# A bias strip on ScalarE's queue, and an output stage finished by column halves: a hybrid decoder layer on one core

## The reference

```python
def _output(h, a_out, b_out, c_out, w_out, g_post):
    y = jnp.concatenate([a_out, b_out, c_out], axis=-1) @ w_out
    return h + _rms_norm(y, g_post)

def _rms_norm(x, g):
    xf = x.astype(jnp.float32)
    y = xf * lax.rsqrt(jnp.mean(xf * xf, axis=-1, keepdims=True) + EPS)
    return (y * g.astype(jnp.float32)).astype(x.dtype)

# before it: u = rms_norm(h, g_pre) @ w_in, split into the inputs of three mixers:
#   A: attention (compressed, selected, window branches) with a relative position bias
#      rel_bias[_t5_bucket(distance)] on every logit
#   B: GLU -> causal depthwise conv of 31 taps -> group norm over channels -> swish -> pointwise
#   C: causal conv of 4 taps -> gates -> linear recurrence over time
```

## Time and profile before

| | us |
|---|---|
| median of 3 runs | 1036.57 (1035.59 to 1037.96) |
| the profiled execution, its own time | 1041.16 |
| its span, first to last instruction | 1039.3 |
| TensorE matmul busy | 949.7 (91%) |
| VectorE busy | 598.8 (58%) |
| ScalarE busy | 374.9 (36%) |

### The profile page before, as it was taken

The page is one execution under the profiler, slowest core; times in us unless marked ns, Lnnn a source line. Parts: engine busy times, 40 slices in busy tenths (PEclk is TensorE's granted clock), DMA queues, the critical chain, the costliest instruction groups (busy, mean ns, idle before and its releaser), DMA issues.

```text
span 1039.3 us, 14529 instructions
## 1 busy us (share of the span) xinstructions
PE 949.7 (91%) x5469; PEld 586.3 (56%) x5469; DVE 598.8 (58%) x1112; ACT 374.9 (36%) x842; POOL 90.7 (9%) x88
## 2 busy tenths in 40 slices
PE   3999999997999999988999999998788989899996
PEld 2665665664666657665666666666454655544442
DVE  4388789999979869754555555577333233212222
ACT  4111253010212010347758667566254454310111
POOL 1011110000001111000020201211311000000000
PEclk9999999998999999999999999999899999999999
DMA  8333641043332554518000000000445755512210
GB/s 301 122 122 114 218 155 40 20 76 87 121 143 93 202 213 142 196 65 271 2 2 2 1 2 1 2 2 1 198 188 226 295 205 213 211 40 81 81 50 31
DMA packets 26734, 117.83 MB, mean 113 GB/s; under 512 B 2809, under 2 KB 11147, under 8 KB 20043
## 3 DMA queue, kind: packets, MB, share of 16 engines
q0 software_dynamic: 7056, 68.16, 17.7%
q1 hardware_dynamic: 18069, 45.75, 13.1%
q10 hardware_dynamic: 1551, 3.14, 1.0%
HBM read 108.07 MB, written 13.29 MB: 117 GB/s over the span
## 4 chain that ended last, share of the span: by engine, by line
PE 71%; DVE 8%; issue 5%; DMA 4%; ACT 4%; DVEq 3%; PEld 3%; SPq 2%; ACTq 0%; POOL 0%; PEldq 0%; POOLq 0%
PE PS L838 23%; PE PS L1825 12%; PE PS L1512 6%; PE PS L1502 6%; PE PS L1525 5%; PE PS L1713 3%; PE PS L1705 3%; PE PS L811 3%; PE PS L1541 2%; DMA main<-in_w_tiles_dram 2%; PEld PS L1757 2%; DVE main L611 2%; DMA main<-in_cmp_v_dram,row 1%; SPq L1030 1%; DVEq L747 1%
## 5 line engine op out<-in xcount | busy, mean ns | idle before, releaser
L838 PE MATMUL PS<-main 128*128 128x352 f32 (+1 forms) x1056 | 332.6, 474 | 7.0 <-DMA main<-in_w_tiles_dram 7.0
L838 PEld LDWEIGHTS PS<-main 128*128 128x128 f32 x1056 | 202.6, 193 | 128.9 <-DMA main<-in_w_tiles_dram 7.6
L1825 PE MATMUL PS<-main 128*128 128x512 f32 (+1 forms) x288 | 125.7, 599 | 0.8 <-DVEq L1689 0.8
L1353 ACT ACTIVATE main<-PS,main 128x512 f32<-128x512 f32 (+3 forms) x192 | 104.4, 566 | 0.7 <-DVE main L1395 0.7
L1345 ACT ACTIVATE main<-PS 128x512 f32<-128x512 f32 (+1 forms) x138 | 73.8, 578 | 77.9 <-PE PS L1512 77.2
L1825 PEld LDWEIGHTS PS<-main 128*128 128x128 f32 (+1 forms) x288 | 53.4, 186 | 72.3 <-issue 72.3
L434 ACT ACTIVATE main<-PS 128x384 f32<-128x384 f32 x24 | 11.8, 490 | 227.6 <-PE PS L838 219.1
L649 DVE SCALAR_TENSOR_TENSOR main<-main,par 128x1022 f32<-128x1022 f32 (+16 forms) x66 | 83.8, 1270 | 5.3 <-issue 0.4
L608 DVE TENSOR_TENSOR main<-main 128x1024 f32<-128x1024 f32 x64 | 75.4, 1220 | 11.7 <-DMA main<-in_cmp_k_dram,row 7.3
L1512 PE MATMUL PS<-cst,main 128*128 128x128 f32 x528 | 76.5, 286 | 3.4 <-ACT main L1353 3.2
L611 DVE TENSOR_TENSOR main<-main 128x1024 f32<-128x1024 f32 (+2 forms) x96 | 75.0, 781 | 7.2
(11 more groups left out here) (305 smaller groups left out, 1058.4 us busy)
## 6 DMA issues: line engine op xcount, KB each, us to landing
main<-in_w_tiles_dram SPq DMA_DIRECT2D x24, 512.0 KB, 4.0
main<-in_x_prompt_dram SPq DMA_DIRECT2D x16, 512.0 KB, 4.8
out_dram<-main SPq DMA_DIRECT2D x12, 512.0 KB, 2.6
main<-in_w_out_dram SPq DMA_DIRECT2D x1, 4096.0 KB, 12.0
diag<-in_win_k_dram SPq DMA_DIRECT2D x8, 256.0 KB, 10.2
diag<-in_win_v_dram SPq DMA_DIRECT2D x8, 256.0 KB, 11.6
out_dram<-in_win_k_dram SPq DMA_DIRECT2D x1, 2016.0 KB
out_dram<-in_win_v_dram SPq DMA_DIRECT2D x1, 2016.0 KB
```

The lines of the kernel that those rows point to most:

```text
L838: last = pe.matmul(bank(3 * s + j)[:, 0:w], ring[:, s, k * P:(k + 1) * P], xT[:, k, t0:t0 + w], start=(k == 0), stop=(k == KD - 1))
L1353: last = act.activation(prob[:, k % 2, g, h * nk_ * P:(h + 1) * nk_ * P], score_set(k, g)[:, h * nk_ * P:(h + 1) * nk_ * P], ACT.Exp, scal ...
L1825: last = pe.matmul(bank(2 * (n % 2) + h)[0:w, :], proj[:, MIX[k], n * P:n * P + w], wo[:, k, h * 512:(h + 1) * 512], start=(k == 0), stop= ...
```

## The change

It has two parts. The strip's store and its skewed read are issued by ScalarE instead of SyncE: the store after the copies of step 3, the read after those of step 5.

The output stage is written anew. The order of tiles is prompt 0 to 6, samples, prompt 7. A prompt tile is signalled, squared, multiplied with `g_post` and finished by halves of 512 columns; the product with `g_post` no longer holds the root and stands ahead of it (into `yb`), and the last operation of a half does the root and the sum with x in one. The sample tile is put on halves of the array's columns: each k has two matmuls of 64 stationary columns, whose results go to partitions 0 to 63 and 64 to 127 of one bank, so that 64 rows x 1024 become 128 x 512. Its sums of squares are then halves of a row's sum on two partitions; four matmuls of one column with pieces of the identity ("fold") add them, between the two halves of the last tile.

```diff
-        def sp_strip(sp):
-            sp.wait_ge(startup_evac, 4)
-            sp.dma_start(scratch["strip"], strip[0:H, :].rearrange("h (o c) -> h o c", o=1).to_broadcast([H, P, SKEW])).then_inc(strip_out, 16)
-
-        def sp_skew(sp):
-            sp.wait_ge(strip_out, 16)
-            sp.dma_start(diag[:, 1:, :], scratch["skewed"]).then_inc(strip_in, 16)
+        def act_strip(act):
+            act.wait_ge(startup_evac, 4)
+            act.dma_start(scratch["strip"], strip[0:H, :].rearrange("h (o c) -> h o c", o=1).to_broadcast([H, P, SKEW])).then_inc(strip_out, 16)
+
+        def act_skew(act):
+            act.wait_ge(strip_out, 16)
+            act.dma_start(diag[:, 1:, :], scratch["skewed"]).then_inc(strip_in, 16)
...
+        OUT = [0, 1, 2, 3, 4, 5, 6, 8, 7]
+        HALVES = [1 if n == NT else 2 for n in OUT]
+        DONE = [sum(HALVES[:m]) for m in range(10)]
...
+            sp.wait_ge(SEM["wvused"], 5)
+            for h in range(2):
+                sp.dma_start(gpost_s[S * h:S * (h + 1), :], dram["g_post"][:, h * 512:(h + 1) * 512].to_broadcast([S, 512])).then_inc(SEM["ld_gp"], 16)
+            for m in range(9):
+                for h, (here, there) in enumerate(x_parts(m, True)):
+                    if h < HALVES[m]:
+                        sp.wait_ge(SEM["y_out"], DONE[m] + h + 1)
+                    sp.dma_start(there, here).then_inc(y_st[m % 3], 16)
...
         def pe_output(pe):
             pe.wait_ge(SEM["ld_wo"], 16)
             pe.wait_ge(SEM["dpair"], 5)
...
+            for m, n in enumerate(OUT):
+                if m >= 2:
+                    pe.wait_ge(SEM["y_gain"], DONE[m - 1])
+                if n < NT:
+                    for h in range(2):
+                        for k in range(KD):
+                            last = pe.matmul(bank(2 * (m % 2) + h), proj[:, MIX[k], n * P:(n + 1) * P], wo[:, k, h * 512:(h + 1) * 512],
+                                             start=(k == 0), stop=(k == KD - 1))
+                        last.then_inc(SEM["y_ps"], 1)
+                        if h == 0 and m > 0 and OUT[m - 1] == NT:
+
+                            pe.wait_ge(SEM["y_sq"], DONE[m])
+                            for o in range(2):
+                                for a in range(2):
+                                    last = pe.matmul(bank(4)[S * o:S * (o + 1), 0:1], ident[:, S * a:S * (a + 1)], ssq[:, 0:1], start=(a == 0), stop=(a == 1))
+                            last.then_inc(SEM["y_fold"], 1)
+                else:
                     for k in range(KD):
...
+                        for h in range(2):
+                            last = pe.matmul(bank(2 * (m % 2))[S * h:S * (h + 1), :], proj[:, MIX[k], T:TOK], wo[:, k, h * 512:(h + 1) * 512],
+                                             start=(k == 0), stop=(k == KD - 1))
+                    last.then_inc(SEM["y_ps"], 1)
...
+                dve.wait_ge(SEM["y_sq"], DONE[m] + 1)
+                if n == NT:
+                    gain(0)
+                    dve.wait_ge(SEM["y_fold"], 1)
+                    dve.tensor_scalar(root, bank(4)[:, 0:1], 1.0 / D, EPS, ALU.mult, ALU.add).then_inc(SEM["y_ms"], 1)
+                else:
+                    one, two = ssq[:, 1 + 2 * (m % 2):2 + 2 * (m % 2)], ssq[:, 2 + 2 * (m % 2):3 + 2 * (m % 2)]
+                    dve.tensor_scalar(root, one, 1.0 / D, EPS, ALU.mult, ALU.add)
+                    gain(0)
+                    dve.wait_ge(SEM["y_sq"], DONE[m] + 2)
+                    dve.drain()
+                    dve.scalar_tensor_tensor(root, two, 1.0 / D, root, ALU.mult, ALU.add).then_inc(SEM["y_ms"], 1)
+                    gain(1)
+                dve.wait_ge(SEM["y_rt"], m + 1)
+                dve.reciprocal(root, root)
+                dve.wait_ge(xo_ld[b], 32 * (m // 3 + 1))
                 dve.drain()
...
+                for h in range(HALVES[m]):
+                    x = xo[:, b, h * 512:(h + 1) * 512]
+                    dve.scalar_tensor_tensor(x, yb[:, m % 2, h * 512:(h + 1) * 512], root, x, ALU.mult, ALU.add).then_inc(SEM["y_out"], 1)
```

More of the change, by code:

```diff
@@ L1785, in program, with x_parts @@
         gpost = late[:, 0:D]
+        gpost_s = late[:, D:D + 512]
         xo = carve(X0, 3 * D).rearrange("p (b n) -> p b n", b=3)
[L1787 to L1796, removed]
+        yb = carve(X0 + 3 * D, 2 * D).rearrange("p (b n) -> p b n", b=2)
+        junk = carve(X0 + 5 * D, 512)
+        OUT = [0, 1, 2, 3, 4, 5, 6, 8, 7]
+        HALVES = [1 if n == NT else 2 for n in OUT]
+        DONE = [sum(HALVES[:m]) for m in range(10)]
+        def x_parts(m, out):
+            n, b = OUT[m], m % 3
+            if n < NT:
+                full = (outs[0][0] if out else dram["x_prompt"])[n * P:(n + 1) * P, :]
+                return [(xo[:, b, h * 512:(h + 1) * 512], full[:, h * 512:(h + 1) * 512]) for h in range(2)]
+            full = outs[1].rearrange("b t d -> (b t) d") if out else dram["x_sample"]
+            return [(xo[S * h:S * (h + 1), b, 0:512], full[:, h * 512:(h + 1) * 512]) for h in range(2)]
         def sp_output(sp):
@@ L1803, in sp_output @@
             sp.wait_ge(SEM["vused"], 4)
[L1804 to L1812, removed]
+            for m in range(3):
+                for here, there in x_parts(m, False):
+                    sp.dma_start(here, there).then_inc(xo_ld[m], 16)
+            sp.wait_ge(SEM["wvused"], 5)
[6 more added lines that the diff above has]
+                    sp.dma_start(there, here).then_inc(y_st[m % 3], 16)
+                if m + 3 < 9:
+                    sp.wait_ge(y_st[m % 3], 32 * (m // 3 + 1))
+                    for here, there in x_parts(m + 3, False):
+                        sp.dma_start(here, there).then_inc(xo_ld[m % 3], 16)
             for b in range(3):
-                sp.wait_ge(y_st[b], 48)
+                sp.wait_ge(y_st[b], 96)
         def pe_output(pe):
@@ L1829, in act_output @@
+                    last.then_inc(SEM["y_ps"], 1)
         def act_output(act):
             act.wait_ge(SEM["vused"], 4)
[L1831 to L1834, removed]
+            for m, n in enumerate(OUT):
+                for h in range(HALVES[m]):
+                    act.wait_ge(SEM["y_ps"], DONE[m] + h + 1)
                     act.drain()
[L1836 to L1839, removed]
+                    sq = ssq[:, 0:1] if n == NT else ssq[:, 1 + 2 * (m % 2) + h:2 + 2 * (m % 2) + h]
+                    act.activation(junk, bank(2 * (m % 2) + h), ACT.Square, accum_out=sq).then_inc(SEM["y_sq"], 1)
+                act.wait_ge(SEM["y_ms"], m + 1)
+                act.activation(rstd[:, m:m + 1], rstd[:, m:m + 1], ACT.Sqrt).then_inc(SEM["y_rt"], 1)
@@ L1856, in program, with gain @@
-        yb = carve(X0 + 4 * D, 2 * D).rearrange("p (b n) -> p b n", b=2)
+            dve.wait_ge(SEM["ld_gp"], 48)
+            for m, n in enumerate(OUT):
+                b = m % 3
+                root = rstd[:, m:m + 1]
+                def gain(h):
+                    g = gpost_s if n == NT else gpost[:, h * 512:(h + 1) * 512]
+                    dve.tensor_tensor(yb[:, m % 2, h * 512:(h + 1) * 512], bank(2 * (m % 2) + h), g, ALU.mult).then_inc(SEM["y_gain"], 1)
+                dve.wait_ge(SEM["y_sq"], DONE[m] + 1)
[14 more added lines that the diff above has]
+                dve.wait_ge(xo_ld[b], 32 * (m // 3 + 1))
+                dve.drain()
+                for h in range(HALVES[m]):
+                    x = xo[:, b, h * 512:(h + 1) * 512]
+                    dve.scalar_tensor_tensor(x, yb[:, m % 2, h * 512:(h + 1) * 512], root, x, ALU.mult, ALU.add).then_inc(SEM["y_out"], 1)
```

25 lines of the change are left out of this document (4 added, 21 removed).

## The result

The changed kernel took 1029.14 us (median of 12 runs, 1024.96 to 1033.34), the kernel before 1037.38 beside it (12 runs, 1033.80 to 1044.88): ratio 0.9907, 95% interval 0.9882 to 0.9932. It is faster, by 0.9%. A ratio compares runs of the kernel's faster state alone, and need not be the quotient of the medians beside it. The forecast of 1029.8 was hit. In the trace the output stage came out near its price; the strip's price of 0 held for the profile it was read from, and not for others of the same kernel.

What follows compares the result with a forecast made beforehand. The prediction took VectorE's convolution to bound the projections and TensorE the output stage. Strip 0, TensorE's output work -5.86, tail -0.96 and last store 0 sum to -6.8 us: from 1036.57 to 1029.8, range 1026.8 to 1033.0.

Steps and rivals of the forecast that it cites:

- Part one: 0: Projections: moving the strip's transfers removes TensorE's 7.04 us weight-tile wait but gains 0, because VectorE's convolution covers it.
- the price without the cover, 9.2: Projections: without VectorE's convolution as cover, removing the tile wait would gain 9.2 us, 7.0 of wait and 2.2 of clock.
- it can move by 0.1 us at most: Third var matmul, issued at 290.27 behind a chunk ending at 290.25; VectorE frees its bank at 290.17, limiting any gain.
- Its +1.6: Part one's upper bound: the new wait lowers TensorE's clock again in the last chunk before 296.6, costing up to 1.6 us.
- The new wait: Projections, at `pe_mean`: TensorE waits about 4 us for VectorE at 257 to 261, in place of the tile wait.
- the last two rivals: Projections' clock: low again in the last chunk, 1031.4 us (chance 0.04); or at 1.2 GHz through the new waits, 1055.5 (0.02).
- The sign by which the forecast was to be wrong: Projections: VectorE's long wait for L884 ending more than 0.5 us away from 297.2 would show the forecast wrong.
- The sample tile: -6.65: Output stage: matmuls on two column halves run together, so the sample tile takes 7.18 us instead of 13.83.
- the rule of the Trainium skill: Output stage rival: column halves overlap partly, 1.59 times, sample tile 8.7 us, kernel 1031.3 us; chance 0.06.
- The fold: +0.79: Output stage, TensorE: four added matmuls, 8 instructions, cost 0.49 plus 0.30 us for the array's shape; bounds 0.3 and 1.28.
- The tail: -0.96: From the last tile's square to the last store's issue: 3.37 us instead of 4.33, including 0.20 for hops.
- The last store: 0: From the last store's issue to the span's end: no change from 3.35 us, bounds -0.7 and +0.35.

Runs made afterwards that it cites:

- e3: The kernel before with 10 of the 31 taps of convolution B left out, strip still on SyncE's queue; 1048.42 us, 1.0018 of the kernel before.
- e4: The kernel before with 10 of 31 convolution B taps left out and the strip's two transfers on ScalarE's queue; 1037.00 us, 0.9883 of the kernel before.
- e2: The changed kernel with the strip's two transfers back on SyncE's queue, so the new output stage alone; 1037.94 us, 0.9920 of the kernel before.
- e11: The kernel before, unchanged, profiled again; 37.31 us from L721 to the end of VectorE's long wait, against 36.32 in the first profile.
- e12: The kernel before, unchanged, profiled once more; 37.01 us from L721 to the end of VectorE's long wait, span 1052.6 us.
- e1: The kernel before with only the strip's two transfers moved to ScalarE's queue, output stage as before; 1041.25 us, 0.9954 of the kernel before.
- e9: The changed kernel, unaltered, run and profiled again on another chip; 1039.18 us, 0.9936 of the kernel before there (1045.29).
- e5: The changed kernel with both halves of the sample tile on the same 64 columns of TensorE; 1046.24 us, 0.9966 of the kernel before.
- e7: The changed kernel with TensorE's wait for the last decode pair moved from the output stage's start to the sample tile; 1035.37 us, 0.9885 of the kernel before.

## Why the prediction was right, step by step

**Part one: 0.** Right in the profile it was made from (36.32 and 36.30), and the price without the cover, 9.2, was right (9.1 in e3 and e4), its clock part by two errors: two of the four chunks behind the wait have 384 columns (5.16 us from start to start, against 4.73 for 352), so at full clock the 64 instructions take some 19.9, not 19.6, and 1.9 was lost, not 2.2; but e3's wait was 7.31, not 7.04. Wrong as a statement on the kernel: the step "it can move by 0.1 us at most" was read from a tie of 290.27 against 290.25, and e2, e11 and e12 show TensorE late by 0.7 to 1.8 there. The prediction allowed 0.1 for it, as a bound, and the mean of 0.9 belongs in the sum. (Its +1.6 was for a slower kernel by the clock, another matter.) The cover had no margin at all, and a tie in one execution should have been priced as a wait in others.

**The new wait.** Expected as one of about 4 us at 257 to 261. It came as three, 2.06, 2.39 and 0.65. The low clock behind them, which the last two rivals were about, did come (6.25 for the chunk at 268.02 instead of 4.90), but TensorE had slack there. The sign by which the forecast was to be wrong, VectorE's long wait ending over 0.5 us away from 297.2, did appear, at 294.14. It was badly chosen: a time on the clock carries whatever varies ahead of it, and the same row stands at 294.38 in e1, 294.50 in e11 and 297.69 in e9. Counted from L721 it did not move.

**The sample tile: -6.65.** 7.02 us measured, 7.18 forecast. By the rule of the Trainium skill ("TensorE: Matmul & The Clock Gate", "Measured speedup vs the span model") it would have been 8.7, an estimate from a figure for three column tiles of 32 columns; this case's run does not agree: 13.88 us with one group of columns (e5) over 7.02 with two is 1.98 times, the ideal but for 1%. Three column tiles no run here has.

**The fold: +0.79.** Mis-sized: 0.34 from its start to the next matmul's. Another 0.4 lies in the two prompt halves on either side of it (7.06 and 7.13 us, against 6.89, an 18th of e1's 123.98). TensorE in all: from 123.98 to 1018.57 - 900.72 = 117.85, -6.13, where -5.86 was forecast.

**The tail: -0.96.** 4.33 went to 3.14, -1.19. The parts were right (0.79 to the join, 0.69, 1.41), but on VectorE the next operation starts before the row of the last one ends: the product 0.08 after the join's start, the reciprocal 0.60 after the product's. The 0.2 added for hops was not there.

**The last store: 0.** 3.35 went to 2.89, -0.46, within the bounds -0.7 and +0.35. The first half's store was on its way by then.

**The sum.** -6.8 was forecast; the terms as measured are -0.9 - 6.1 - 1.2 - 0.5 = -8.7. The ratios of the two comparisons, 0.9907 and 0.9936, are -9.6 and -6.7 us, with intervals of some 2.6 and 3.8 to either side, and hold it. The -6.8 of the forecast lies inside the second and just outside the first (-7.1 to -12.2). The forecast of 1029.8 came closer to 1029.14 than its terms deserve: they were 1.9 short, and the kernel before was at 1037.38 in the comparison, 0.8 over the median on which the forecast was built. That the number was hit this closely is luck of the chip, too: +-1.2 for the scatter was taken from three runs, while the kernel before ran from 1033.80 to 1044.88 in the comparison and had medians of 1045.29 to 1048.84 on the other chips, where the changed kernel's 1039.18 (e9) lies outside 1026.8 to 1033.0. What carries over is the difference.

## What to carry to other kernels

A stall on an engine that another one covers is worth its price minus the cover, and where the two are equal within a few per cent the profile of one execution cannot say which: price it as a mean, or look at several. Half-width matmuls gain only when two of them stand side by side on different columns; then they cost half. And the tail behind the last matmul is worth splitting: the first half's work goes under the second half's matmuls, and the first half's store under the finishing operation.

## What the runs showed that I had not expected

The runs of the kernel before spread over 15 us on one chip. In the profiles the spread lies in two places, some 10 us ahead of decode and some 10 in the decode pairs, whose equal work takes 40.7 to 44.4 us by how long TensorE's clock stands at its half level (3.4 us or 10) behind waits of 0.5 to 2.4 us in a stretch of small matmuls. What decides between the two was not found. A gain of 1 or 2 us, as e7's may be, is lost in that. A store of 1536 KB from 8 partitions held the weight tiles behind it on its own queue (34.59 us), but issued from ScalarE's queue it delayed no tile on SyncE's: no wait for a tile stands in any of the profiles with the strip there.
